# MLP up projection by seven block products in passes 1 to 7: a two-layer encoder step in fp32

## The reference

```python
D_MODEL = 1024
D_FF = 4 * D_MODEL

def sq_relu_mlp(x, w_up, w_down):
    return jnp.square(jax.nn.relu(x @ w_up)) @ w_down

hp = hp + sq_relu_mlp(rmsnorm(hp, norm_ffn[i]), ffn_w_up[i], ffn_w_down[i])
hs = hs + sq_relu_mlp(rmsnorm(hs, norm_ffn[i]), ffn_w_up[i], ffn_w_down[i])
```

## Time and profile before

| | |
|---|---|
| median of 3 runs | 2913.31 us (2912.53 to 2919.41) |
| profiled execution, its own time | 2915.13 us |
| its span, first to last instruction | 2913.3 us |
| granted PE clock, mean | 0.993 |
| PE busy | 2827.7 us, 97% |
| DVE busy | 1669.8 us, 57% |
| ACT busy | 1174.4 us, 40% |
| POOL busy | 546.1 us, 19% |
| one pass of mlp1 | 94.2 us, of it 50.56 up and 43.64 down |

### The profile page before, as it was taken

One profiled execution on the slowest core, in us unless ns is written; L12 is line 12 of the kernel. 1 busy time (PEld: TensorE's weight loads), 2 busy tenths in 40 slices (PEclk: granted clock), 3 DMA queues, 4 the chain that ended last, 5 costly groups with the idle time before them and its releaser, 6 DMA issues. The chain is left out here.

```text
span 2913.3 us, 44219 instructions
## 1 busy us (share of the span) xinstructions
PE 2827.7 (97%) x17111; PEld 2582.3 (89%) x17111; DVE 1669.8 (57%) x2534; ACT 1174.4 (40%) x2199; POOL 546.1 (19%) x481
## 2 busy tenths in 40 slices
PE   8999999889999999999999999989999999999998
PEld 8889877569989998899989899987998999889997
DVE  4389789942565456654652266537156644665465
ACT  3377568771433333333331144433143333333332
POOL 2222111102201010110112244446220111011110
PEclk9999999999999999999999999999999999999999
DMA  4422622243210111101104333356321101110111
GB/s 149 110 63 80 162 54 45 44 130 111 69 53 16 57 58 43 58 14 58 56 3 150 110 99 97 103 184 236 115 74 44 44 29 58 43 58 14 58 44 65
DMA packets 196038, 222.59 MB, mean 76 GB/s; under 512 B 27745, under 2 KB 172065, under 8 KB 195890
## 3 DMA queue, kind: packets, MB, share of 16 engines
q1 hardware_dynamic: 195746, 220.05, 23.9%
q10 hardware_dynamic: 144, 0.52, 0.1%
HBM read 170.58 MB, written 49.95 MB: 76 GB/s over the span
## 5 line engine op out<-in xcount | busy, mean ns | idle before, releaser
L982 PE MATMUL acc_e<-end_xT_hi,early 128*128 128x384 f32 x752 | 254.5, 338 | 0.0
L982 PE MATMUL acc_e<-end_xT_lo,end_w_hi 128*128 128x384 f32 x752 | 254.0, 338 | 0.0
L982 PE MATMUL acc_e<-end_xT_hi,end_w_hi 128*128 128x384 f32 x752 | 252.5, 336 | 1.4 <-ACT mlp_hid L850 1.4
L982 PE MATMUL acc<-mid_xT_hi,mid_w_hi 128*128 128x384 f32 x752 | 251.4, 334 | 1.1 <-ACT mlp_hid L850 1.1
L982 PE MATMUL acc<-mid_xT_hi,mid_w_lo 128*128 128x384 f32 x752 | 251.3, 334 | 0.0
L982 PE MATMUL acc<-mid_xT_lo,mid_w_hi 128*128 128x384 f32 x752 | 251.2, 334 | 0.0
L1118 DVE TENSOR_TENSOR h<-mlp_dn_acc,h 128x512 f32<-128x512 f32 x308 | 205.6, 686 | 77.9 <-PE mlp_dn_acc L993 75.9
L946 POOL TENSOR_TENSOR mid_w_lo<-spare_w,mid_w_hi 128x1024 fp32r<-128x1024 f32 x32 | 79.8, 2494 | 645.7 <-ACT mid_w_hi L837 601.1
L464 PE MATMUL acc<-mid_w_hi,mid_xT_hi 128*128 128x256 f32 x648 | 191.0, 295 | 6.6 <-PEq L572 3.8
L1105 DVE TENSOR_TENSOR mlp_h_lo<-mlp_hid,mlp_h_hi 128x1024 fp32r<-128x1024 f32 x92 | 139.1, 1511 | 99.5 <-ACT mlp_h_hi L865 98.8
L865 ACT ACTIVATE mlp_h_hi<-mlp_hid 128x1024 fp32r<-128x1024 f32 x92 | 97.6, 1061 | 237.5 <-PE mlp_dn_acc L993 162.4
(11 more groups left out here) (466 smaller groups left out, 8027.9 us busy)
## 6 DMA issues: line engine op xcount, KB each, us to landing
spare_w<-in_ffn_w_up SPq DMA_DIRECT2D x32, 1024.0 KB, 7.3
mlp_dn_raw<-in_ffn_w_down SPq DMA_DIRECT2D x16, 1024.0 KB, 7.0
proj_w_raw<-in_a_w_in SPq DMA_DIRECT2D x8, 1024.0 KB, 6.1
mid_w_raw<-in_ffn_w_down SPq DMA_DIRECT2D x8, 1024.0 KB, 5.0
end_w_raw<-in_ffn_w_down SPq DMA_DIRECT2D x8, 1024.0 KB, 4.9
spare_w<-in_b_w_in SPq DMA_DIRECT2D x6, 1024.0 KB, 5.9
mid_w_raw<-in_b_w_in SPq DMA_DIRECT2D x6, 1024.0 KB, 6.4
hd<-h SPq DMA_DIRECT2D x9, 512.0 KB, 8.8
```

Source lines behind the costliest of these rows:

```text
L982: mm = pe.matmul(up_acc[:, u % 2, 0:GW], up_s[a][:, k, f % 2 * P:(f % 2 + 1) * P], x_s[c][:, k, g * GW:(g + 1) * GW], start=(n == 0), stop ...
```

## The change

The up stage of passes 1 to 7 is done by seven block products too. x (1024 columns by 1152 rows, transposed in SBUF) is cut into 2 by 2 blocks of 512 by 576, the pass's w_up into 2 by 2 blocks of 512 by 256. Each product (`up_product`) has four units of 12 matmuls with 288 rows moving. The results go to two groups of four PSUM banks (`bank_a`, `bank_b`), the second made of the two banks of `up_acc` and the two that were for transposes; products 2, 4 and 6 are added by PE onto what the bank holds. DVE adds the results to the four blocks of `hid` (20 instructions, 128x288), and ACT does Relu and Square behind it (`finished`), in place.

The sums of x blocks (S1 to S4) are made by DVE in pass 0 (`x_sum`). S1 stays in SBUF. S2, S3 and S4 are stored to a DRAM tensor `x_sums` and loaded in each pass in two halves of 128x1152; ACT and DVE split each half again (`x_hi`, `x_low`) into the place of one x block. The four sums of weights (`up_sum`), and the low halves of the up weights (`up_low`, seven in a pass), are made by DVE; POOL's part falls away in passes 1 to 7. All products, up and down, now share the ring of two slots for weights, and pass 0's up stage stays as it was, apart from DVE's new work beside it. The weights come in 512 KB pieces, each when its buffer is free.

The diff, cut to what the text speaks of:

```diff
+    def units(i):
+        return 4 * NP * i + (UU - pre - 4 * NP)
+
+    def sums(i):
...
+
+    def copies(i):
+        return 8 * i - 8
+
+    def squares(i):
...
+        pool_w = b.sb("pool_w", [P, 3 * D + XH])
+        B11u, B12u, B21u, B22u, T1u, T2u = pool_w[:, 0:D], pool_w[:, D:2 * D], R[2], pool_w[:, 2 * D:3 * D], R[0], R[1]
+        B11, B12, B21, B22, T1 = R[0], R[1], R[2], R[3], pool_w[:, 3 * D:4 * D]
+        s3 = as_dn(B22u)
+        x_land, s2_land = pool_w[:, 3 * D:3 * D + XH], pool_w[:, 0:XH]
+        hid = b.sb("hid", [P, FC, TOK])
+        xs = b.sb("xs", [P, 2, KH, TH], F32R)
...
+        psT = b.ps("psT", [P, 2, 512])
+        bank_a = [dn_acc[:, t, 0:C] for t in range(TB)]
+        bank_b = [up_acc[:, 0, 0:C], up_acc[:, 1, 0:C], psT[:, 0, 0:C], psT[:, 1, 0:C]]
...
+        first_k, second_k, early_rows, late_rows = slice(0, KH), slice(KH, KB), slice(0, TH), slice(TH, TOK)
+        x_s = (sh.xhi, sh.xlo)
+        streamed = [z[:, first_k, early_rows] for z in x_s]
+        X11, X12, X22 = ([z[:, ks, rows] for z in x_s] for ks, rows in ((first_k, late_rows), (second_k, late_rows), (second_k, early_rows)))
+        X_OF = (streamed, X11, X12, streamed, X22, [xs[:, 0, :, :], xs[:, 1, :, :]], streamed)
+        C11, C12, C21, C22 = hid[:, 0:2, TH:TOK], hid[:, 2:4, TH:TOK], hid[:, 0:2, 0:TH], hid[:, 2:4, 0:TH]
...
-        W_OF = (B11, B21, B11, B12, B21, t1[:, :, :], B22)
+        UP_W_OF = (T2u, B11u, B21u, B12u, B21u, T1u, B22u)
+        W_OF = (B11, B21, B11, B12, B21, T1, B22)
...
+                def ahead(i):
+
+                    sp.wait_ge(x_lo_done, x_no(i, "S2", 0))
+                    load_x("S2", 1, s2_land)
+                    sp.wait_ge(x_lo_done, x_no(i, "S2", 1))
...
+                def alongside(i, last):
+                    sp.wait_ge(up_sum_done, 4 * i)
+                    load_dn(B12, i, 0, 1, b12_in)
+                    sp.wait_ge(x_lo_done, x_no(i, "S3", 0))
+                    load_x("S3", 1, x_land)
+                    sp.wait_ge(w_lo_done, w_up_no(i, 0))
+                    load_dn(B22, i, 1, 1, b22_in)
+                    sp.wait_ge(x_lo_done, x_no(i, "S3", 1))
+                    load_x("S4", 0, x_land)
+                    sp.wait_ge(w_lo_done, w_up_no(i, 4))
+                    load_dn(B21, i, 1, 0, b21_in)
+                    sp.wait_ge(x_lo_done, x_no(i, "S4", 0))
+                    load_x("S4", 1, x_land)
+                    sp.wait_ge(w_lo_done, w_up_no(i, 5))
+                    load_dn(B11, i, 0, 0, b11_in)
                     if not last:
-                        sp.wait_ge(w_lo26_done, (NP - 2) * i + NP - 2)
...
+                def finished(i, block, j, n, at):
+
+                    dst = block[:, j, :]
+                    act.wait_ge(summed, sums(i) + n)
+                    act.activation(dst, dst, ACT.Relu).then_inc(relued, 1)
+                    act.wait_ge(relued, 6 * i - 6 + at)
+                    square(dst)
...
+                        sample(i, f, squares(i) + 2)
+                    act.wait_ge(up_done, units(i) + 16)
+                    weights(ring_hi[0], T1u)
+                    x_hi(i, "S4", 0, x_land)
+                    for f in range(2):
+                        finished(i, C21, f, 10 + 2 * f, 1 + f)
+                    x_hi(i, "S4", 1, x_land)
+                    act.wait_ge(up_done, units(i) + 20)
+                    act.wait_ge(b22u_in, 16 * i)
+                    weights(ring_hi[1], B22u)
+                    act.wait_ge(squared, squares(i) + 4)
...
+                    for f in range(2):
+                        finished(i, C22, f, 14 + 2 * f, 3 + f)
...
+                    else:
+                        act.wait_ge(b11_in, 16 * (i + 1))
+                        weights(ring_hi[0], B11)
+                        act.wait_ge(squared, squares(i) + 6)
+                        hidden(1, A12)
+                    for f in range(2):
+                        finished(i, C12, f, 18 + 2 * f, 5 + f)
+                    act.wait_ge(up_done, units(i) + 28)
+                    act.wait_ge(b22_in if last else b21_in, 16 * (i + 1))
+                    weights(ring_hi[1], B22 if last else B21)
+                    for f in range(2, FC):
+                        sample(i, f, squares(i) + 8)
+                    if not last:
+                        x_hi(i, "S2", 0, s2_land)
...
+                def up_product(i, k):
+
+                    slot, xk, onto = (k + 1) % 2, X_OF[k], k in (2, 4, 6)
+                    w = [as_up(ring_hi[slot]), as_up(ring_lo[slot])]
+                    pe.wait_ge(w_lo_done, w_up_no(i, k))
+                    if k in (0, 3, 6):
+                        pe.wait_ge(x_lo_done, 6 * i + (2 * (k // 3 + 1) - 6))
+                    for u in range(4):
+                        f, c = u // 2, u % 2
+                        if k == 0:
+                            pe.wait_ge(added, DU * i - ADDS[NP - 1] + u + 1)
+                        elif k == 1 and u == 0:
+                            pe.wait_ge(added, DU * i)
+                        elif k == 3:
+                            pe.wait_ge(copied, copies(i) + (u + 1))
+                        elif k == 5:
+                            pe.wait_ge(copied, copies(i) + (u + 5))
+                        elif onto:
+                            pe.wait_ge(summed, sums(i) + ({2: 0, 4: 4, 6: 12}[k] + u + 1))
+                        dst, n = (bank_a, bank_b, bank_b, bank_a, bank_a, bank_b, bank_b)[k][u], 0
+                        for kk in range(KH):
+                            for a, x in TERMS:
+                                mm = pe.matmul(dst, w[a][:, kk, f * P:(f + 1) * P], xk[x][:, kk, c * C:(c + 1) * C],
+                                               start=(n == 0 and not onto), stop=(n == KH * len(TERMS) - 1), skip_group_check=onto)
+                                n += 1
+                        mm.then_inc(up_done, 1)
+
...
+                def x_low(i, what, half, land):
+                    dve.wait_ge(x_hi_done, x_no(i, what, half))
+                    dve.tensor_tensor(x_to(1, half), x_half(land), x_to(0, half).bitcast(F32), ALU.subtract).then_inc(x_lo_done, 1)
...
+                def x_sum(m):
+
+                    what, q = X_PIECES[m]
+                    r, before, lo = x_raw[m % XR], x_raw[(m - 1) % XR], x_raw[XR]
+                    n = X_RAW[m] - X_STEPS[what]
+                    old = m - XR
+                    if old >= 0 and old in X_STORED:
...
+                    elif what == "S2":
+                        dve.tensor_tensor(r, before, x_of(0, 0, False, q), ALU.subtract).then_inc(x_step, 1)
+                        dve.wait_ge(x_step, n + 1)
+                        dve.tensor_tensor(r, r, x_of(1, 0, False, q), ALU.subtract).then_inc(x_step, 1)
...
+                    adds(i, 0, first)
+                    x_low(i, "S2", 0, s2_land)
...
+                        if k == 2:
+                            dve.wait_ge(s_done, 4 * i + 3)
+                            dve.wait_ge(h_lo_done, NP * i + 2)
+                            h_sum(A12, A12, A11)
+                            dve.wait_ge(w_sum_done, 4 * i + 3)
+                            dve.wait_ge(w_lo_done, w_dn_no(i, 1))
+                            w_sum(B21, B21, B11)
+                            x_low(i, "S2", 1, s2_land)
...
+                        dve.wait_ge(up_done, units(i) + (13 + u))
+                        dve.tensor_tensor(cols_of(C22, u), bank_a[u], cols_of(C12, u), ALU.add).then_inc(summed, 1)
+                    sample_low(i, 0)
+                    sample_low(i, 1)
+                    up_low(i, 5)
+                    x_low(i, "S4", 0, x_land)
+                    if last:
+                        u_into_h(2, 3)
+                    for u in range(4):
+                        dve.wait_ge(up_done, units(i) + (17 + u))
+                        dve.tensor_tensor(cols_of(C21, u), bank_a[u], cols_of(C12, u), ALU.add).then_inc(summed, 1)
+                    x_low(i, "S4", 1, x_land)
+                    up_low(i, 6)
...
+                    else:
                         hidden_low(NP * i + 1, 0, A11)
-                        sample_low(i, 1)
-                        hidden_low(NP * i + 2, 1, A21)
-                        weight_low(NP * i + 3, quarters(up_lo, 0), B11.rearrange("p f (q c) -> p f q c", c=P), quarters(up_hi, 0))
+                        dve.wait_ge(squared, squares(i) + 4)
+                        dve.wait_ge(w_lo_done, w_up_no(i, 6))
+                        h_sum(s3, A11, A21)
+                    for u in range(4):
+                        dve.wait_ge(summed, sums(i) + (5 + u))
+                        dve.wait_ge(up_done, units(i) + (21 + u))
+                        dve.tensor_tensor(cols_of(C22, u), bank_b[u], cols_of(C22, u), ALU.add).then_inc(summed, 1)
...
+                    else:
+                        dve.wait_ge(b11_in, 16 * i + 16)
+                        dve.wait_ge(b12_in, 16 * i + 16)
+                        w_sum(T1, B12, B11)
```

(78 more changed lines are left out.)

545 lines of the change are left out of this document (329 added, 216 removed).

## The result

The changed kernel takes 3029.73 us (median, 3025.98 to 3033.07) against 2914.73 us for the kernel before, a ratio of 1.0392 with a 95% interval of 1.0374 to 1.041: 3.9% slower. The forecast was 2990 us in a range of 2940 to 3040. Its profiled execution spans 3031.3 us, 118.0 more than the one before.

What follows compares the result with a forecast made beforehand. PE, busy 97% of the span, was taken to bound the kernel. 2915.1 us + 48 (middle passes, waits less PE's saving) + 15 (pass 0) + 14 (clock) = 2992; forecast 2990, range 2940 to 3040.

Steps and rivals of the forecast that it cites:

- PE's saving: Up stage of passes 1 to 7: 336 matmuls at 132.8 ns, 5.9 us less a pass, 83 us over 14 passes.
- (A): Before up product 6 in each middle pass: PE waits for DVE's first add of product 5 into C22, 1.9 us.
- (B): Before down product 1 in each middle pass: PE waits for product 0's adds on DVE, 4.4 us.
- (C): Before down product 3 in each middle pass: PE waits for DVE's first add of product 2, 3.4 us.
- The clock term: Falls to half clock after PE's idle times, where no later wait covers them: +7 us a layer, +14.
- Rival 4: Clock falls at (B) and (C) in every pass, 2.4 us each, all on PE's path: 3045 us, chance 0.10.
- The x reload: Loads of x halves in passes: 3.7 us each, leaving a 0.2 us wait before up product 3.
- Rival 5: Queued x reloads take 7.3 us instead of 3.7, up to 3.6 less 0.9 at (A): about 3030 us, chance 0.05.
- The middle passes: Six a layer: 9.9 us of waits against 5.9 saved, +4.0 us a pass, +48 us in two layers.
- Pass 0: PE waits 3.3 us for hidden's high halves and low half, 7.5 us in all with later waits; +15 in two layers.
- pass 7: Saves 5.9 us, waits about 2.0 at (A) and 3.5 before its down stage: counted as 0.
- Rival 1: ACT and DVE overlap better than laid out, PE waits at most 2 us a pass: about 2875 us, chance 0.10.

Runs made afterwards that it cites:

- e9: Changed kernel plus matmuls that nothing reads in PE's waits of passes 1 to 7 (14, 25, 26, last group ahead of the weights wait): 3015.97 us.
- e6: Changed kernel with ACT's list reordered: B11's rounding between the halves of C22's finish, B21's between those of C12's: 3004.24 us.
- e3: Changed kernel with A11's low half and the sum s3 placed behind C22's adds in DVE's list: 3009.48 us.
- e4: Changed kernel with S2's halves and B21's difference one to three products later, the up sums one later: 3013.77 us.
- e7: Changed kernel with the load of S3's second half ahead of B12's load in SyncE's list: 3007.42 us.
- e8: Changed kernel with the reorderings of e3, e4, e6 and e7 together, plus B12's difference and A12's low behind C12's adds: 2907.4 us.

## Why the prediction was near, and 40 us short

**PE's saving was right in layer 1 and somewhat high in layer 0.** 132.8 ns was forecast for 288 columns and 132.7 measured, so PE gains 5.9 us a pass in layer 1, as forecast. The forecast took layer 1's times for both layers; in layer 0 the kernel before has shorter passes:
```profile
861.63:911.57 49.94, 49.94 (x289) 49.94 (x288) 18.73 (x13) 19.14 (x38) 7.28 (x3) 1.00 0.07 22
911.57:955.13 43.56, 43.56 (x193) 36.05 (x193) 34.56 (x44) 12.48 (x16) 2.69 (x1) 1.00 0.20 73
```
There the saving is 49.9 - 44.6 = 5.3 us, so the sum is 79 us and not 83.

**The waits (A), (B), (C) were right in place, and nearly in size.** (A) was 1.85 us for a forecast of 1.9, and (B) at full clock 4.21 in layer 1 and 4.35 in layer 0 for 4.4. (C) at full clock was to be 3.4; e9 shows 2.9 and e6 2.74 and 2.95, so it was forecast 0.5 us too long. (A) and (C) vanish when their causes do (e3, e4). The cause of (B) was half right: the sum had ACT's steps in it, but the forecast also called (B) DVE's own gapless list. DVE's rows show 1.85 and 2.98 us of idle time for ACT inside it, and e6 takes 2.4 us off (B) by ACT's order alone.

**The clock term was too small, and right only by its number.** +14 was forecast for all falls: those after (B) as far as (C) does not cover them, and the end of passes 0 and 7. e9 gives 14 for passes 1 to 7 alone, 12 of it in the twelve middle passes, and the falls of pass 0 come on top. That (C) swallows part of the fall after (B) was right: it shrinks from 2.74 to 1.61 us, 1.1 of the 1.5 to 3.1 us that the 24 slow matmuls cost. The trace also shows falls after (A)'s 1.85 us, in half of the middle passes, which (B) swallows whole. That an idle time of 1.92 us at 358 us had brought no fall was no proof for 1.85 us elsewhere. Rival 4, all falls at full price, 3045, is out.

**The x reload was mis-sized.** The wait before up product 3 was to be 0.2 us and is 1.1 to 1.3. Its term took 3.7 us for a load; S3's second half is issued between two 512 KB loads and takes 5.43. The forecast had named another load, S4's second half, as the tightest. e7 moves S3's and gains 22 us, so this one place goes with more than half of the miss: 14 us by the wait itself, the rest for reasons that stay open. Rival 5 had this mechanism at 7.3 us, but priced it at (A).

**The middle passes were mis-sized by these together.** The six middle passes, from their first up matmul to that of pass 7, before and after, in layer 0 and layer 1:
```profile
861.63:1422.67 561.04, 561.04 (x2882) 515.95 (x2880) 319.73 (x342) 189.73 (x324) 59.80 (x24) 1.00 0.13 45
2239.66:2804.73 565.07, 565.07 (x2880) 519.47 (x2880) 319.82 (x342) 189.54 (x324) 59.93 (x24) 1.00 0.13 45
...
873.98:1477.41 603.43, 553.22 (x3170) 497.07 (x3168) 444.27 (x564) 243.04 (x318) 0.00 (x0) 0.96 0.24 77
2314.57:2921.57 607.00, 558.47 (x3169) 497.18 (x3168) 444.54 (x564) 242.99 (x318) 0.00 (x0) 0.96 0.23 77
```
They take 42.4 and 41.9 us more, 7.1 and 7.0 a pass, where +4.0 and a part of the clock's 14 were forecast. Of the difference of 3 us, 1.0 is the wait for x and 1.0 the clock (e9); in layer 1 another 1.0 is the spacing of 232 in place of 227 ns (192 matmuls), in layer 0 0.6 the smaller saving. What is left, (C)'s 0.5 the other way included, is 1 us a pass or less and was not taken apart. Together the middle passes hold 84 of the 118 us.

**Pass 0 and pass 7 were mis-sized too.** Of the other 34 us pass 0 takes 12 in layer 0 and 11 in layer 1, pass 7 takes 6 and 1, and the phases between the two MLPs take 4. For pass 0 15 were forecast, for the rest nothing but the clock's share. In pass 0 PE waits 4.72 us (layer 0) and 4.24 (layer 1) for hidden's low half, where 3.3 was worked out. The forecast had DVE's sums of x end 6 us before the up stage. In layer 1 they end at 2258.3 us, 2.2 us before it, and the chain into that wait goes from the store of a sum through DVE's last sums and lows:
```profile
2253.82 2.22 DMA x_sums<-mlp_pool_w
...
2262.26 1.14 DVE mlp_pool_w L1331
2263.39 1.15 DVE early L1325
2264.54 0.14 issue
2264.67 7.11 PE mlp_dn_acc L1192 x24
```
The 24 matmuls after it take 7.11 us instead of 5.49, a fall with no cover. No run took pass 0's share apart, and the causes in pass 7 and in the phases between stay open.

**Rival 1, overlap, was wrong for this order and right in kind:** e8 brings the pass under its 94 us by order alone, to 91.5 in layer 0 and 91.8 in layer 1. The layout was right for the written order; what the forecast did not weigh is that the order could be changed. It stays over the 88.3 us of PE's own work. The twelve middle passes gain 26 us on the kernel before, and the rest of the kernel, pass 0 above all, loses 18 of them, so only 8 us arrive.

## What to carry to other kernels

Seven products for eight save time only as far as VectorE's extra sums do not stand ahead of an accumulator's add that TensorE waits for. Lay out the lists of all engines with measured durations before judging such a change: here the same instructions in another order are worth 122 us, which is more than the 79 that the change takes from TensorE. In each list, put first what another engine waits for next, and what is merely due soon behind it; that holds for SyncE's loads as well, where taking one 512 KB load from ahead of a needed one gained 22 us. A filler for idle time must stand ahead of every wait of its place and be no longer than the wait, or it delays what it is to help.
